# Three units in place of two, chunk by chunk, at the start of four layers

## The reference, cut to what matters

```python
def _rmsnorm(x, g):
    y = x32 * lax.rsqrt(jnp.mean(x32 * x32, axis=-1, keepdims=True) + RMS_EPS)
    return (y * g.astype(jnp.float32)).astype(x.dtype)

def _swiglu(x, w_gate, w_up, w_down):
    return (jax.nn.silu(x @ w_gate) * (x @ w_up)) @ w_down

h = _rmsnorm(x, norm_gains[i, 2])
h = _swiglu(h, ffn_w_gate[i], ffn_w_up[i], ffn_w_down[i])
x = x + _rmsnorm(h, norm_gains[i, 3])
```

## Time and profile before

| | |
|---|---|
| median of 3 runs | 1454.95 us (1453.6 to 1456.08) |
| the profiled execution | 1454.11 us, of which the span of the trace is 1452.2 us |
| PE busy | 97% of the span |
| DVE / ACT / POOL busy | 72% / 50% / 15% |
| mean granted TensorE clock | 0.991 of full speed |

### The profile page before, as it was taken

How to read it: one execution, slowest core, us unless ns; L and a number is a source line. 1 busy time by engine, 2 the same in 40 slices (tenths; PEclk the granted TensorE clock), 3 DMA queues, 4 the chain that set the end, 5 groups by cost and what they waited for, 6 DMA issues and landing times.

```text
span 1452.2 us, 31327 instructions
## 1 busy us (share of the span) xinstructions
PE 1413.3 (97%) x11890; PEld 1343.7 (93%) x11890; DVE 1047.8 (72%) x1635; ACT 733.1 (50%) x1191; POOL 218.9 (15%) x232
## 2 busy tenths in 40 slices
PE   8999999999999999999999999999999999999997
PEld 6999999999986899999878888899999998999997
DVE  7988799987986878874687965677764456677753
ACT  4447555554446655564366443554344446544442
POOL 0000133310000123321000010113320000133300
PEclk9999999999999999999999999999999999999999
DMA  9874377796880446665432300346665442466662
GB/s 375 293 263 175 102 233 240 257 397 249 322 298 1 160 128 187 180 223 181 159 102 83 117 7 2 112 136 189 184 211 188 140 135 90 137 190 189 207 201 69
DMA packets 68432, 258.18 MB, mean 178 GB/s; under 512 B 7545, under 2 KB 9857, under 8 KB 67970
## 3 DMA queue, kind: packets, MB, share of 16 engines
q1 hardware_dynamic: 68354, 257.10, 53.2%
HBM read 256.01 MB, written 1.06 MB: 177 GB/s over the span
## 4 chain that ended last, share of the span: by engine, by line
PE 80%; DVE 11%; ACT 3%; DMA 3%; issue 2%; SPq 0%; ACTq 0%; DVEq 0%
PE ps L721 20%; PE ps L723 20%; PE ps L722 20%; PE ps L596 3%; PE ps L738 2%; DVE lo L1792 2%; DMA modfirst_b<-in_wmod 2%; PE ps L682 1%; DVE modraw L1798 1%; DMA modlate<-in_wmod 1%; PE ps L684 1%; PE ps L683 1%; ACT hi L1284 1%; DVE U L2341 1%; PE ps L745 1%
## 5 line engine op out<-in xcount | busy, mean ns | idle before, releaser
L1792 DVE TENSOR_TENSOR lo<-raw,hi 128x1024 fp32r<-128x1024 f32 (+1 forms) x350 | 474.8, 1373 | 182.2 <-ACT hi L1284 181.6
L721 PE MATMUL ps<-OH,lo 128*128 128x256 f32 x1984 | 561.5, 283 | 3.0 <-DVE lo L1792 3.0
L723 PE MATMUL ps<-OH,hi 128*128 128x256 f32 x1984 | 558.4, 281 | 0.0
L722 PE MATMUL ps<-OL,hi 128*128 128x256 f32 x1984 | 553.9, 279 | 0.0
L1284 ACT ACTIVATE hi<-raw 128x1024 fp32r<-128x1024 f32 (+1 forms) x350 | 380.5, 1111 | 15.1 <-PE ps L723 9.9
L721 PEld LDWEIGHTS ps<-OH,lo 128*128 128x128 f32 x1984 | 372.9, 188 | 8.3 <-DVE lo L1792 6.2
L722 PEld LDWEIGHTS ps<-OL,hi 128*128 128x128 f32 x1984 | 374.4, 189 | 0.0
L723 PEld LDWEIGHTS ps<-OH,hi 128*128 128x128 f32 x1984 | 372.7, 188 | 0.0
L722 PE MATMUL ps<-GL,hi 128*128 128x256 f32 x704 | 195.2, 277 | 0.0
L723 PE MATMUL ps<-GH,hi 128*128 128x256 f32 x704 | 195.2, 277 | 0.0
L721 PE MATMUL ps<-GH,lo 128*128 128x256 f32 x704 | 195.2, 277 | 0.0
(11 more groups left out here) (378 smaller groups left out, 1958.4 us busy)
## 6 DMA issues: line engine op xcount, KB each, us to landing
raw<-in_w SPq DMA_DIRECT2D x288, 512.0 KB, 3.8
raw<-in_w SPq DMA_DIRECT2D x64, 704.0 KB, 5.4
modraw<-in_wmod SPq DMA_DIRECT2D x77, 512.0 KB, 5.7
modlate<-in_wmod SPq DMA_DIRECT2D x6, 512.0 KB, 5.3
modlast<-in_wmod SPq DMA_DIRECT2D x5, 512.0 KB, 4.9
modfirst_a<-in_wmod SPq DMA_DIRECT2D x4, 512.0 KB, 11.2
modfirst_b<-in_wmod SPq DMA_DIRECT2D x4, 512.0 KB, 12.0
l<-in_lora_in SPq DMA_DIRECT2D x1, 1536.0 KB, 6.1
```

The costliest lines, as they stand in the source:

```text
L721: pe.matmul(bank[:, 0:T], lo[:, r, w], oh[:, k0 + k], start=first, stop=False)
L722: pe.matmul(bank[:, 0:T], hi[:, r, w], ol[:, k0 + k], start=False, stop=False)
L723: ins = pe.matmul(bank[:, 0:T], hi[:, r, w], oh[:, k0 + k], start=False, stop=final)
L1792: dve.tensor_tensor(lo[:, s, 0:kt * P], raw[:, s, 0:kt * P], hi[:, s, 0:kt * P].bitcast(F32), ALU.subtract).then_inc(lo_made, 1)
```

## The change

`two_units` becomes `first_units(name, units, ...)`, and `together` a number. It stays 2 in the layers that had it, and is 3 in `first_layer`. There the sums come after chunks 1, 2, 3 (two), 4 (two) and 5 (two), and the spread comes between the three units and unit 3. So that unit 2's weights are ready, ACT and DVE convert them in the last step of the layer ahead (`third=True` in ffn0_down, rw_out, glu0_down, sgu_out): ACT between `hi` of unit 1 and the last evacuation, DVE after `lo` of unit 1. `early_weights` then converts unit 3 only, and DVE leaves out step 0 of the next layer (`made=1`).

```diff
-            def two_units(name, oh, ol, fresh, after_chunk, beside):
+            def first_units(name, units, oh, ol, fresh, after_chunk, beside):
...
-                    for r in range(2):
+                    for r in range(units):
                         pe.matmul(PS[r][:, 0:T], lo[:, r, w], oh[:, k], start=(k == 0), stop=False)
...
                 def after_chunk(r, k):
-                    if r == 0 and k >= 2:
-                        stat(k - 2)
-                    if r == 2 and k == 2:
-                        spread_inverse(("x", n), 1)
+                    for c in ((), (0,), (1,), (2, 3), (4, 5), (6, 7), (), ())[k]:
+                        ins = stat(c)
+                        if c == DC - 1:
+                            ins.then_inc(S("xstat_done"), 1)
 
                 def between(i, r):
                     if isinstance(i, int) and i == 0 and r == 0:
-                        stat(DC - 2)
-                        stat(DC - 1).then_inc(S("xstat_done"), 1)
-                layer(name, OH, OL, between, fresh=True, after_chunk=after_chunk, together=True)
+                        spread_inverse(("x", n), 1)
+                layer(name, OH, OL, between, fresh=True, after_chunk=after_chunk, together=3)
...
@@ ACT
                         elif nxt and not hold:
                             weights_hi(name, i, r, nxt)
+                        if third and last and r == SLOTS - 1:
+                            weights_hi(name, i, SLOTS, nxt)
                         evacuate(i, r, start + 4 * i + r)
...
-            layer("rw_out", with_square(4, False, par_gain("norm_g2", DC)))
+            layer("rw_out", with_square(4, False, par_gain("norm_g2", DC)), third=True)
             residual(4)
-            early_weights("rw_out", 2)
+            early_weights("rw_out", 2, 1)
...
@@ DVE
                         elif nxt and not hold:
                             weights_lo(name, i, r, nxt)
+                        if third and last and r == SLOTS - 1:
+                            weights_lo(name, i, SLOTS, nxt)
                         if evacuate:
                             evacuate(i, r, start + 4 * i + r)
...
-                layer(name, evacuate, peel_first=True)
+                layer(name, evacuate, peel_first=True, made=1)
...
-            layer("att_v", values_out, peel_all=True)
+            layer("att_v", values_out, peel_all=True, made=1)
```

More of the change, by code:

```diff
@@ L699, in body @@
                 def body(i, last):
[L700 to L703, removed]
+                    ahead = together if isinstance(i, int) and i == 0 else 0
+                    if ahead:
+                        first_units(name, ahead, oh, ol, fresh, after_chunk, beside)
+                        for r in range(ahead):
                             if between and start:
                                 between(i, r)
-                    for r in range(2 if both else 0, SLOTS):
+                    for r in range(ahead, SLOTS):
                         u = start + 4 * i + r
@@ L789, in out_layer @@
                 else:
-                    layer(name, oh, ol, between, together=(TILES[name] == KT))
+                    layer(name, oh, ol, between, together=2 if TILES[name] == KT else 0)
                     pe.wait_ge(S("sq_added"), (DC - 2) * n)
@@ L852, in _ @@
             keep_busy(3, 7)
-            layer("ffn0_up", OH, OL, together=True)
+            layer("ffn0_up", OH, OL, together=2)
             out_layer("ffn0_down", GH, GL, 1, 9)
@@ L1284, in weights_hi, with early_weights, layer @@
                 act.activation(hi[:, s, 0:kt * P], raw[:, s, 0:kt * P], ACT.Copy).then_inc(hi_made, 1)
-            def early_weights(name, count):
-                for r in range(SLOTS, SLOTS + count):
+            def early_weights(name, count, first=0):
+                for r in range(SLOTS + first, SLOTS + count):
                     weights_hi(name, COUNT[name] // SLOTS - 1, r, KT)
-            def layer(name, evacuate, peel_first=False, hold=False, peel_all=False, made=0):
+            def layer(name, evacuate, peel_first=False, hold=False, peel_all=False, made=0, third=False):
                 start, kt, nxt = START[name], TILES[name], next_tiles(name)
@@ L1505, in _ @@
             conv_ffn_up("ffn0_up", 0)
-            layer("ffn0_down", with_square(1, True, own_gain(1)))
+            layer("ffn0_down", with_square(1, True, own_gain(1)), third=True)
             residual(1)
-            early_weights("ffn0_down", 2)
+            early_weights("ffn0_down", 2, 1)
             scaled_hi(2, lambda c: col("kv_norm_g", c))
@@ L1772, in _ @@
                 act.activation(OH[:, c], Us_[:, c], ACT.Copy).then_inc(S("oh_ready"), 1)
-            layer("sgu_out", with_square(6, False, par_gain("norm_g2", 5 * DC)))
+            layer("sgu_out", with_square(6, False, par_gain("norm_g2", 5 * DC)), third=True)
             residual(6)
-            early_weights("sgu_out", 2)
+            early_weights("sgu_out", 2, 1)
             scaled_hi(7, lambda c: col("norm_g2", 6 * DC + c))
@@ L1803, in early_weight, with layer @@
                 weights_lo(name, COUNT[name] // SLOTS - 1, SLOTS, KT)
-            def layer(name, evacuate=None, peel_all=False, peel_first=False, hold=False, ahead=None, made=0, last_riders=True):
+            def layer(name, evacuate=None, peel_all=False, peel_first=False, hold=False, ahead=None, made=0, last_riders=True, third=False):
                 start, kt, nxt = START[name], TILES[name], next_tiles(name)
@@ L2111, in _ @@
             gate_gain(1, 3 * DC)
-            layer("ffn0_down", peel_all=True)
+            layer("ffn0_down", peel_all=True, third=True)
             residual(1, par_gain("kv_norm_g", 0))
@@ L2487, in _ @@
                                       ).then_inc(operand_ready, 2)
-            layer("rw_out")
+            layer("rw_out", third=True)
             residual(4, par_gain("norm_g2", 2 * DC))
             glu_up("glu0_up", 5)
-            layer("glu0_down")
+            layer("glu0_down", third=True)
             residual(5, par_gain("norm_g2", 4 * DC))
@@ L2506, in gating_out @@
                     gelu_input(k, START["sgu_v"])
-            layer("sgu_v", gating_out, peel_all=True)
+            layer("sgu_v", gating_out, peel_all=True, made=1)
             for g in range(2):
@@ L2543, in _ @@
             low_part(Us_, OH, OL, DC - 1)
-            layer("sgu_out")
+            layer("sgu_out", third=True)
             residual(6, par_gain("norm_g2", 6 * DC))
```

22 lines of the change are left out of this document (10 added, 12 removed).

## The result

The changed kernel takes 1458.78 us (median of 20 runs, 1453.79 to 1464.18) against 1455.39 us for the kernel before in the same sessions (20 runs, 1450.16 to 1462.37): a ratio of 1.0030, 95% interval 1.0017 to 1.0043, which is +4.4 us (2.5 to 6.2); the two medians themselves lie 3.4 apart. The profiled execution took 1456.02 us, its span 1454.2.

The account below looks back on a forecast made before the run. The prediction took PE, busy 97% of the span, to bound the kernel. Terms of 0.99 + 0.99 + 1.76 + 1.76 = 5.50 us on the 1454.95 median gave 1460.4 us, range 1457.5 to 1462.3.

Parts of the forecast that it names:

- att_v: At unit 4 PE would wait 0.91; an unbroken DVE queue passes on the full shift: +1.76 us, or 0.9 if loads absorb it.
- Part 3: Inverse spread 15 matmuls later at four starts: DVE's copy and what follows shift 1.76 us, costing 5.50 us in sum.
- GLU layers: glu0_up and glu1_up: PE waits for unit 4's low weights, +0.99 us each.
- the 1.28 us: Time from the start of a lo to the first matmul waiting for it, used to compute the unit 4 waits.
- sgu_v: DVE and ACT take turns without final slack: unit 4 waits 1.45 us, the full shift comes through, +1.76 us.
- rival 2: Part of the shift is absorbed, att_v costing 0.9 as DMAs set attention's entry: +3.6 to 4.8 us; chance 0.22.
- Part 1: Three units chunk by chunk at the starts: same work, no operand waits; value 0, -0.1 to +0.1 us per start.
- Part 2: Unit 2's weights converted in the layer ahead: value 0, or 0 to 0.2 us at each of rw_out and sgu_out.
- rival 3: The shift moves bursts against the clock gate and a stretch loses its clock: 1462 to 1463.5 us; chance 0.08.
- the rule of the Trainium skill cited in the prediction: Waits between matmul bursts lower the clock, next burst at half speed; new waits would then cost more than their length.
- rival 5: Faster: the two-unit pass waits for operands at chunks 1 to 3; 0.9 us a start, 1451.4 us; chance 0.04.

Follow-up runs that it names:

- the late spread alone: The kernel before with only the spread moved to after unit 2, two units and no early weights; ratio 1.0043, +6.3 us.
- part 2 alone: The changed kernel's early weights with TensorE's order, sums and spreads as in the kernel before; ratio 0.9986, and 0.9987 when run again.

## Why the prediction was right, and where not

**Direction and size.** +5.5 us was forecast. The stages show +5.5 in the first trace, 7.6 in the second and 5.4 with the late spread alone; the ratios say +4.4 (2.5 to 6.2), +5.2 (3.2 to 7.3) and +6.3 (4.2 to 8.3). The forecast of 1460.4 stands 1.6 over the measured 1458.78, within the range. Added to the 1455.39 of before in 20 runs it would have been 1460.9, 2.1 over. And the agreement of the sums is partly luck: two terms were 0.25 too small each, and att_v's was 0.4 too large in the first trace and 1.7 too small in the second.

**Part 3, the mechanism: right.** Spread at 12.24 after the first matmul (forecast 12.22); DVE's copy 12.88 after it where before it was 11.11, so 1.77 later (forecast 1.76); `lo` of unit 4 at 15.20, where it was 13.42. The kernel before with the late spread alone loses as much or more.

**GLU layers: term mis-sized, 1.24 for 0.99.** The step that failed was the 1.28 us from the start of a `lo` to the first matmul that waits for it. I took it from sgu_v's unit 6. In glu0_up it is 1.47 (967.32 to 968.79). The `lo` is not what is longer: alone it takes 1.23 us here as there, and `lo_made` counts up 1.24 after its start in both layers. What is longer is TensorE's side, from that count to the first matmul: 0.23 us in glu0_up and glu1_up, 0.04 in sgu_v and att_v. The first `lo` alone, then the first weight load of unit 4 in glu0_up and in sgu_v, all of the changed kernel:

```profile
967.32 1.23 DVE L1791 TENSOR_TENSOR lo<-raw,hi 128x1024 fp32r<-128x1024 f32 x1 [0.47 <-ACT hi L1281]
```

```profile
968.76 0.19 PEld L721 LDWEIGHTS ps<-OH,lo 128*128 128x128 f32 x1 [1.17 <-issue]
...
1164.81 0.19 PEld L721 LDWEIGHTS ps<-OH,lo 128*128 128x128 f32 x1 [1.50 <-DVE lo L1791]
```

In sgu_v, where the units are written out one by one, the weight load itself waits for `lo`. In the GLU layers unit 4 is the first unit of a loop (`bodies` puts it into a `Fori`), and two more of TensorE's queue instructions stand between `lo_made` (968.56) and the load: one at 968.59 and one at 968.69, the wait of L717. Every wait at unit 4 of a GLU layer has this 0.23 or more, in five kernels of these experiments, and every one in sgu_v and att_v has 0.04. No run writes the loop out, so that the loop is the reason is read from the rows and not tested. Of the 0.25 that were missing 0.19 are this, and the rest is the restart of the matmuls after a wait (0.20 from the first to the second, where 0.12 is usual).

POOL's low part of the GLU output runs beside these `lo`, from 967.60 for 1.54 us. It lengthens the second `lo` and not the first: 2.90 for the two, where two take 2.36 at 945.18, of which 1.76 is the second, begun while POOL ran. The Trainium skill, page SBUF — State Buffer, section Who interferes with whom, says that a VectorE instruction with two inputs in SBUF contends with a GpSimd instruction that reads SBUF. The second `lo` agrees, with 0.53 us more; the first began before POOL's instruction, and 0.95 us beside it cost it nothing. TensorE doesn't wait for the second at unit 5, so this contention is no part of the missing 0.25.

**sgu_v: right.** 1.46 at unit 4 (forecast 1.45), three small ones of 0.15 behind it (0.3 was expected), and the stage 1.76 to 1.85 longer, in both traces and with the late spread alone (59.60, 59.69, 59.68).

**att_v: right up to att_q, open behind it.** Unit 4 waits 0.92 (forecast 0.91), and from the reciprocal at 346.21 to the matmul at 410.20 it is 63.99 where it was 62.23: the full 1.76, through an unbroken DVE queue. Behind that, loads decide, as rival 2 said. In the first trace of after 0.4 us is absorbed (1.38), in the second the shift doubles (84.83 is 3.4 to 3.6 more). There DVE waits for a load in front of the bias, and the scores for the bias, in DVE's and PE's timeline of the changed kernel run again:

```profile
427.71 1.23 DVE L1797 SCALAR_TENSOR_TENSOR modlate<-modlate,cond 128x1024 f32<-128x1024 f32 x1 [1.67 <-DMA modlate<-in_wmod]
```

```profile
431.27 0.49 PE L877 MATMUL ps<-K,Q 64*128 64x128 f32 x4 [2.67 <-DVE bias L2150]
```

With the late spread alone the stage is 1.1 to 1.2 longer (82.48). So the term is 1.1 to 3.6 and not one number.

**Part 1: the reading of the profile right, the value wrong.** No wait for an operand within two units, none within three. But "value 0" holds only as long as the late spread hides the other condition. DVE needs the inverse and the finished products; a pass over three units finishes units 0 and 1 only at its end, after 72 matmuls and not 48. Once the spread is early this costs 0.5 to 0.7 us at the GLU and sgu_v starts. I had asked who waits for the inverse, and not what else the same instruction waits for.

**Part 2: the narrow covers held.** ACT's second `hi` ends at 946.10, and the evacuation still waits 0.18 for PE; DVE's second `lo` ends at 947.54, and the reciprocal follows at 947.64, 0.29 after the root, as before. Forecast 0.2 and 0.1 of room, found so. That part 2 alone measured some 2 us faster twice, with the interval's end at 1.000, I had not forecast. The traces explain about 0.1 at sgu_out and 0.2 to 0.4 at the attention's entry; the remainder stays open, and it may be chance.

**The clock (rival 3): not borne out.** The waits at unit 4 cost their length and no clock. Busy time of the changed kernel in the stretches around those of glu0_up and sgu_v; the figure behind the five engines is the granted clock:

```profile
966.00:972.00 6.00, 5.00 (x43) 4.83 (x42) 4.64 (x8) 3.65 (x6) 2.25 (x3) 1.00 0.31 94
1162.00:1168.00 6.00, 4.71 (x38) 4.31 (x37) 2.94 (x4) 2.96 (x5) 0.00 (x0) 1.00 0.23 87
```

1.00 is the 2.4 GHz level. I had read the rule of the Trainium skill cited in the prediction as making more of these waits than their length. For waits of 1.15 and 1.46 us in dense matmuls these rows don't bear that reading out, and the section's own example is of longer waits, for loads, so the reading went further than the page.

**Faster (rival 5): right about the mechanism, wrong about its threshold.** I said that it decides from a start over a microsecond earlier. With 0.86 earlier, two units already lose 0.33 of it, at the third chunk and not at the first. With three units for the first chunks and 6 keep_busy, TensorE does come to chunk 0 before its operand.

## What to carry to other kernels

Before moving a small step that opens a queue (here a spread of reciprocals), count the matmuls put in front of it and compare with the slack of the first unit that needs that queue's output: 15 matmuls against 0.8 us of slack decided this case. Going through several units chunk by chunk also delays the end of the first of them, and with it whoever takes its products. Limiting it to the chunks whose operands are short removed that wait, but by the stages it was no better here than two units with early sums. A longer stretch of ready work is worth something only if the start is moved up with it, and moving the start stops paying where the first operand itself is late. A price taken from one wait holds for another only if the waiting engine's queue looks the same there: the 1.28 us of a written-out layer were 1.47 at the head of a loop.

## What the runs showed of the hardware that I had not expected

**Two paces at one clock.** In the down layers a chunk of three matmuls takes 340 ns in some executions and 353 in others, layer by layer, with the granted clock at 1.00 in both. ACT's evacuations in glu0_down come every 7.77 us in the profiled execution of before, and every 7.48 in another one of the same kernel; over the layer's 16 units of 11 chunks that is 2.3 us. In order of time, ACT of before, then of before run again:

```profile
1096.29 0.39 ACT L1338 ACTIVATE SQ<-ps 128x256 f32 x1 [4.48 <-PE ps L723]
1104.07 0.39 ACT L1338 ACTIVATE SQ<-ps 128x256 f32 x1 [4.49 <-PE ps L723]
```

```profile
1097.39 0.38 ACT L1338 ACTIVATE SQ<-ps 128x256 f32 x1 [4.18 <-PE ps L723]
1104.87 0.38 ACT L1338 ACTIVATE SQ<-ps 128x256 f32 x1 [4.19 <-PE ps L723]
```

The two executions of the kernel with early weights alone differ in the same way: the stage with glu1_down is 196.05 in one and 194.49 in the other. In glu0_up a unit takes 2.81 us in some executions and 2.83 in others, 0.7 to 0.8 us over the layer, and not always together with glu0_down. That is why the changed kernel with the spread after the seventh chunk has a stage of 194.25 with glu0_up, below the kernel before, though it waits 0.42 there; with glu1_up it has 194.99. I have no cause for it.

**The clock differs between executions of one program.** Busy time by stretch around the first scores (the figure after the engines is the granted clock), of after and of the same kernel run again:

```profile
424.00:440.00 16.00, 14.06 (x95) 10.75 (x94) 10.93 (x25) 9.35 (x32) 0.00 (x0) 1.00 0.55 198
```

```profile
424.00:440.00 16.00, 12.31 (x74) 9.15 (x73) 9.64 (x20) 6.51 (x20) 0.00 (x0) 0.89 0.62 226
```

A mean of 0.89 over 16 us is some 3.5 us at the 1.2 GHz level, (1 - 0.89) x 16 x 2, and the other execution had none. In six executions that I compared at four such places (around 155, 432, 512 and 712 us), the mean over 16 us lies between 0.68 and 1.00, and differs between executions of one program. These differences and the two paces amount to several microseconds between executions; how much of the spread of some 10 us between runs of one kernel they make was not worked out. They are why the stages, and not two spans, show what a change of 5 us does.
